# Hybrid decoder step: the last normalization in one pass with early aggregation, its rows stored in 16 pieces of 256 KB by the queues of SyncE and ScalarE in turn

## The reference, cut to what matters

```
def layer_norm(x, g, b):
    xf = x.astype(F32)
    mu = jnp.mean(xf, -1, keepdims=True)
    var = jnp.mean(jnp.square(xf - mu), -1, keepdims=True)
    return ((xf - mu) * lax.rsqrt(var + LN_EPS) * g.astype(F32) + b.astype(F32)).astype(x.dtype)
...
    f, fbuf = conv_ffn(h, ffn_buf, ffn_w_up, ffn_conv_w, ffn_w_down)
    y = layer_norm(DN_ALPHA * h + f, ln2_g, ln2_b)
```

## Time and profile before

| | |
|---|---|
| time, three runs | 2946.45, 2952.71, 2958.77 us; median 2952.71 |
| profiled execution, span | 2947.1 us; the page gives no other time for it |
| TensorE busy in the span | 2788.9 us, 95% |
| VectorE, ScalarE, GpSimd busy | 77%, 47%, 12% |
| the chain that ended last | 49% TensorE, 5% VectorE |

### The profile page before, as it was taken

The page is one execution under the profiler, slowest core; times in us unless marked ns, Lnnn a source line. Parts: engine busy times, 40 slices in busy tenths (PEclk is TensorE's granted clock), DMA queues, the critical chain, the costliest instruction groups (busy, mean ns, idle before and its releaser), DMA issues.

```text
span 2947.1 us, 55566 instructions
## 1 busy us (share of the span) xinstructions
PE 2788.9 (95%) x22685; PEld 2676.0 (91%) x22685; DVE 2278.0 (77%) x3537; ACT 1384.8 (47%) x2371; POOL 359.2 (12%) x332
## 2 busy tenths in 40 slices
PE   8999999999989969999889999999999999999996
PEld 8999999988888658889889999999999999999996
DVE  6656877877657777755688888888888888878898
ACT  4434545545646544522264444444444453434344
POOL 0010000013370315223330000000000000000002
PEclk9999999999989989999999999999999999999998
DMA  7564444448722884563344444444343464434343
GB/s 221 179 206 107 117 119 128 113 150 286 275 82 105 343 247 117 148 175 92 90 157 136 119 126 117 137 115 132 111 141 111 137 194 163 153 112 155 114 124 118
DMA packets 521474, 440.14 MB, mean 149 GB/s; under 512 B 36264, under 2 KB 476767, under 8 KB 515147
## 3 DMA queue, kind: packets, MB, share of 16 engines
q1 hardware_dynamic: 456662, 300.70, 35.6%
...
...
## 4 chain that ended last, share of the span: by engine, by line
PE 49%; DVE 5%; issue 1%; ACT 1%; POOL 1%; DMA 1%; DVEq 0%; ACTq 0%; POOLq 0%
PE i L3363 42%; PE i L140 7%; DVE f_half L3869 1%; DMA x_blocks<-s_blk 1%; POOL x_blocks L3311 1%; DVE x_blocks L3907 1%; DVE h_rows L3902 0%; DVE y_rows L4000 0%; DVE w_ring L3858 0%; DVE x_blocks L3835 0%; PE i L3372 0%; DVE y_rows L3993 0%; DVE f_sum L3862 0%; DVE ln_parts L3913 0%; ACT x_blocks L3657 0%
## 5 line engine op out<-in xcount | busy, mean ns | idle before, releaser
L3363 PE MATMUL i<-x_blocks,f_half 128*128 128x272 f32 x10752 | 1357.0, 288 | 26.0 <-DVE h_rows L3902 10.9
L3363 PEld LDWEIGHTS i<-x_blocks,f_half 128*128 128x128 f32 x10752 | 1347.0, 189 | 31.7 <-DVE x_blocks L3907 14.1
L570 PE MATMUL a<-xb_in,w_half 128*128 128x272 f32 x4200 | 546.9, 291 | 8.9 <-DVE w_half L972 4.6
L570 PEld LDWEIGHTS a<-xb_in,w_half 128*128 128x128 f32 x4200 | 536.0, 190 | 18.2 <-issue 7.2
L3586 ACT CAST f_half<-w_ring 128x1024 fp32r<-128x1024 f32 (+2 forms) x370 | 346.2, 936 | 403.1 <-PE i L3363 339.5
L3869 DVE TENSOR_TENSOR f_half<-w_ring,f_half 128x1024 fp32r<-128x1024 f32 (+2 forms) x362 | 393.4, 1087 | 80.3 <-ACT f_half L3586 77.9
L3869 DVE TENSOR_TENSOR f_half<-f_sum,f_half 128x1024 fp32r<-128x1024 f32 (+2 forms) x148 | 159.5, 1078 | 81.4 <-ACT f_half L3586 81.4
L972 DVE TENSOR_TENSOR w_half<-w_ring,w_half 128x1024 fp32r<-128x1024 f32 x129 | 157.5, 1222 | 82.9 <-ACT w_half L708 82.5
L3586 ACT CAST f_half<-f_sum 128x1024 fp32r<-128x1024 f32 (+2 forms) x148 | 138.8, 938 | 150.1 <-PE i L3363 148.9
L3323 POOL TENSOR_TENSOR f_half<-w_ring,f_half 128x512 fp32r<-128x512 f32 x8 | 12.9, 1611 | 1397.0 <-ACT f_half L3586 1397.0
L708 ACT CAST w_half<-w_ring 128x1024 fp32r<-128x1024 f32 x125 | 131.3, 1050 | 108.9 <-PE a L570 104.8
...
## 6 DMA issues: line engine op xcount, KB each, us to landing
...
```

The costliest lines, as they stand in the source:

```text
L570: last = nc.tensor.matmul(ps[bank][:, 0:HT2], half(q, w)[:, k], XB[v[j]][:, k], start=j in (0, 1, 3) and k == 0 and i == 0, stop=k == HK - ...
L3363: last = nc.tensor.matmul(ps[bank][:, 0:HT2], half(e, j, wl_)[:, s], XB[:, x0 + s, xl_, BLK_OF[j]], start=start and s == 0 and i == 0, sto ...
```

## The change

- Gamma is multiplied into `y_rows` before the statistics are complete, by blocks: GpSimd does it for blocks 0 to 13 (two at a time, 128 x 4 x 256 elements, `times_g` of GpSimd), in pairs 2 to 7 of the last quarter and once after them; VectorE does the last two blocks in the tail. The statistics are taken from the rows before that.
- y = y*gamma*rstd + (beta - mean*rstd*gamma). The bracket is a product of a matrix with six rows: ones, the shift -mean*rstd, and their halves, against beta and gamma and theirs. TensorE makes it, 16 matmuls of 128 x 512 into six PSUM banks, and VectorE needs one pass over the rows (L4066 after). For this the shift is transposed on TensorE (four transposes) and copied by ScalarE, and beta and gamma are loaded as two rows (`BG_RAW`), whose halves GpSimd makes in pair 6 (L3355 and L3357 after, 2 x 2048).
- The first ten blocks' statistics are aggregated during the last pair (`early_moments`), and their result is put back as if it were the statistics of one block (`early_tuples`); the final bn_aggr reads 42 columns and not 96.
- The loads of gamma and beta as broadcast rows go four pairs earlier in SyncE's queue.
- The last transposition writes bank 0 and need not wait for the copy of the one before; the statistics of blocks 12 and 13 are taken earlier in the last pair.
- The 512 prompt rows are stored in 16 pieces of 128 x 512; odd column pieces (`ACT_STORES`) are issued by ScalarE, even ones by SyncE. GpSimd does the sample rows only.

```diff
-            V_GROUPS = [[(t, q) for q in range(4)] for t in range(QT - 1)] + [[(QT - 1, 0), (QT - 1, 1)]]
-            P_UNITS = [(QT, 0), (QT - 1, 1), (QT, 1)]
+            P_XG, E_ROWS = KT - 2, 10
+            ACT_STORES = [(t, q) for t in range(QT) for q in (1, 3)]
+
+            def turn_bank(m):
+                return 6 if m < KT - 1 else 0
...
+                    if g == 3 * HK + 3:
+                        sp.wait_ge(xq, 28)
+                        sp.wait_ge(tout, 32 * (FT // 4))
+                        sp.dma_start(GROW, A["ln2_g"].partition_broadcast(P)[:, 0, :]).then_inc(gr_in, 16)
+                        sp.dma_start(BROW, A["ln2_b"].partition_broadcast(P)[:, 0, :]).then_inc(gr_in, 16)
+                    if g == 3 * HK + 5:
+                        sp.wait_ge(tr, 6)
+                        sp.dma_start(BG_RAW[0:1], A["ln2_b"]).then_inc(bg_in, 16)
+                        sp.dma_start(BG_RAW[1:2], A["ln2_g"]).then_inc(bg_in, 16)
...
+                for t in range(QT):
+                    for q in range(4):
+                        if (t, q) in ACT_STORES:
+                            continue
+                        sp.wait_ge(yr, 4 * t + q + 1)
+                        sp.dma_start(O[0][0, t * P:(t + 1) * P, q * Q4:(q + 1) * Q4], YN[:, t, q * Q4:(q + 1) * Q4]).then_inc(y_out, 16)
...
+                def times_g(m):
+                    cols = slice(m * P, (m + 2) * P)
+                    gp.wait_ge(bst, m + 2)
+                    g = GROW[:, cols].rearrange("p (o n) -> p o n", o=1).broadcast_to((P, QT, 2 * P))
+                    nc.gpsimd.tensor_tensor(YN[:, 0:QT, cols], YN[:, 0:QT, cols], g, ALU.mult).then_inc(xg, 1)
+
                 for e in range(NP):
                     for j in range(7):
                         if on_pool(e, j):
                             gp.wait_ge(hq, 7 * e + j + 1)
                             nc.gpsimd.tensor_tensor(half(e, j, 1), source(e, j), half(e, j, 0).bitcast(F32), ALU.subtract).then_inc(lp, 1)
...
+                    i = e - NU - 3 * HK
+                    if i == 2:
+                        gp.wait_ge(gr_in, 32)
+                    if i >= 2:
+                        times_g(2 * (i - 2))
+                    if i == 6:
+                        gp.wait_ge(bg_in, BI0 + 32)
+                        gp.wait_ge(tr, 10)
+                        nc.gpsimd.tensor_copy(BG[0:2, :], BG_RAW[:, :]).then_inc(bg_hi, 1)
+                        gp.wait_ge(bg_hi, BH0 + 1)
+                        nc.gpsimd.tensor_tensor(BG_LO[:, :], BG_RAW[:, :], BG[0:2, :].bitcast(F32), ALU.subtract).then_inc(bg_lo, 1)
+                times_g(KT - 4)
...
+                pe.wait_ge(cp, KT - 1)
+                pe.wait_ge(sh, SH0 + 1)
+                for t in range(QT):
+                    last = nc.tensor.transpose(ps[6][0:6, t * P:(t + 1) * P], SH_T[:, t, :], ident)
+                last.then_inc(sh_t, 1)
...
+                for u in range(4 * QT):
+                    t, q = u // 4, u % 4
+                    if u >= 6:
+                        pe.wait_ge(yr, u - 5)
+                    nc.tensor.matmul(ps[u % 6][:, :], SH[:, t * P:(t + 1) * P], BG[:, q * Q4:(q + 1) * Q4], start=True, stop=True).then_inc(cs, 1)
...
+                act.wait_ge(sh_t, ST0 + 1)
+                nc.scalar.copy(SH[:, :], ps[6][0:6, :]).then_inc(sh_r, 1)
                 act.wait_ge(nm, NM0 + 1)
...
+                for h in range(2):
+                    y = YN[0:NS, QT, half_cols(h)]
+                    nc.scalar.activation(y, y, ACT.Identity, scale=RD[0:NS, QT:], bias=NMR[0:NS, QT:]).then_inc(nz, 1)
+                for t, q in ACT_STORES:
+                    act.wait_ge(yr, 4 * t + q + 1)
+                    nc.scalar.dma_start(O[0][0, t * P:(t + 1) * P, q * Q4:(q + 1) * Q4], YN[:, t, q * Q4:(q + 1) * Q4]).then_inc(y_out, 16)
...
+                        if not more and n in (2, 3, 4):
+                            early_moments(2 * (n - 2), min(2 * (n - 2) + 2, QT + 1))
+                        if not more and n == 4:
+                            early_tuples()
...
-                        nc.vector.scalar_tensor_tensor(y, y, MV[:, t, 0:1], ps[q][:, :], ALU.subtract, ALU.mult).then_inc(lk1, 1)
...
-                        nc.vector.scalar_tensor_tensor(y, y, RD[:, t:t + 1], ps[4 + q][:, :], ALU.mult, ALU.add).then_inc(yr, 1)
...
+                times_g(P_XG + 1)
+                dve.wait_ge(xg, XG0 + P_XG // 2 + 2)
+                for u in range(4 * QT):
+                    t, q = u // 4, u % 4
+                    y = YN[:, t, q * Q4:(q + 1) * Q4]
+                    dve.wait_ge(cs, CS0 + u + 1)
+                    nc.vector.scalar_tensor_tensor(y, y, RD[:, t:t + 1], ps[u % 6][:, :], ALU.mult, ALU.add).then_inc(yr, 1)
```

More of the change, by code:

```diff
@@ L3914, in parts, with early_moments, early_tuples @@
                     last.then_inc(bst, 1)
+                def early_moments(first, to):
+                    for tt in range(first, to):
+                        r = P if tt < QT else NS
+                        last = nc.vector.bn_aggr(MV[0:r, tt], BS[0:r, tt, 0:E_ROWS])
+                    link.link(last)
+                def early_tuples():
+                    n = float(E_ROWS * P // 2)
+                    for k in (0, 3):
+                        nc.vector.memset(BS[:, :, E_ROWS - 1, k:k + 1], n)
+                        nc.vector.tensor_copy(BS[:, :, E_ROWS - 1, k + 1:k + 2], MV[:, :, 0:1])
+                        nc.vector.tensor_scalar(BS[:, :, E_ROWS - 1, k + 2:k + 3], MV[:, :, 1:2], n, None, ALU.mult)
                 row_sums(0)
@@ L3973, in _ @@
                 add_down(NP - 1, 6)
-                for m in range(KT - 3, KT):
+                for m in range(KT - 2, KT):
                     parts(m)
                 dve.wait_ge(bst, KT)
-                for first, to in ((QT - 1, QT + 1), (0, QT - 1)):
-                    for tt in range(first, to):
-                        r = P if tt < QT else NS
-                        last = nc.vector.bn_aggr(MV[0:r, tt], BS[0:r, tt])
-                    last.then_inc(bst, 1)
-                dve.wait_ge(dev, 2)
@@ L3983, in _ @@
[L3983 to L4000 removed]
+                for tt in range(QT + 1):
+                    r = P if tt < QT else NS
+                    parts_ = BS[0:r, tt].rearrange("p m s -> p (m s)")[:, (E_ROWS - 1) * 6:KT * 6]
+                    last = nc.vector.bn_aggr(MV[0:r, tt], parts_)
@@ new lines, in _, with times_g @@
+                last.then_inc(bst, 1)
+                def times_g(m):
+                    cols = slice(m * P, (m + 1) * P)
+                    g = GROW[:, cols].rearrange("p (o n) -> p o n", o=1).broadcast_to((P, QT, P))
+                    nc.vector.tensor_tensor(YN[:, 0:QT, cols], YN[:, 0:QT, cols], g, ALU.mult).then_inc(xg, 1)
+                dve.wait_ge(gr_in, 32)
+                times_g(P_XG)
+                dve.wait_ge(dev, 2)
+                link.link(nc.vector.reciprocal(RD[:], RD[:]))
```

109 lines of the change are left out of this document (45 added, 64 removed).

## The result

The changed kernel takes 2962.04 us (median of 5 runs, 2956.74 to 2964.74). The kernel before, run beside it, takes 2951.94. The ratio is 1.0031, with a 95% interval of 1.0018 to 1.0044: about 9 us slower, within the 0.5% that the prediction called no change. The forecast was 2961.3.

What follows compares the result with a forecast made beforehand. TensorE was taken to set the pace in the pairs, with VectorE nearly full (1.07 us to spare). Then +13.1 us up to the last bn_stats and -4.5 in the tail gave +8.6 on 2952.7: 2961.3 us, range 2947 to 2970.

Steps and rivals of the forecast that it cites:

- Hold of VectorE's two-input instructions: Pairs 2 to 5: GpSimd's gamma pieces block VectorE instructions with two SBUF inputs; 0.9 us each, +3.6.
- GpSimd gets there first, and holds it: After a pair's bn_stats, GpSimd's gamma piece starts before VectorE's two-input tensor_tensor and delays it: +2.1 us of VectorE time.
- Pair 6 with the clock: Pair 6: gamma piece, copy and subtraction on GpSimd delay product 6, +7.2 us; TensorE's clock drop adds +1.5.
- Pair 7 and the step before the last bn_stats: Pair 7: held instruction and early aggregations, +1.4 us; before the last bn_stats, no wait for ScalarE's copy, -0.6.
- The tail: From the last bn_stats to the span's end: 20.0 us instead of 24.5, -4.5 (bounds -3 and -6).
- They keep up, with nothing to spare: Tail stores: 16 pieces of 256 KB every 0.66 us need 397 GB/s, against the 401 the queues reached.
- about two: End of the tail: microseconds from GpSimd's last store issue, at 17.9, to landing, so the end is near 20.
- rival C: Tail stores don't keep up: 2 KB rows at a tenth less rate, tail 1.5 us longer, 2962.8 us; 8%.
- signs of being wrong: Listed before measuring: those tensor_tensor at 0.67 us throughout, pairs that still take 11.95, or first stores that queue.
- ends last: Tail: GpSimd's sample rows finish near 20 us, after VectorE's side at 18.8, and so set the end.
- Rival A: Pairs: no hold, GpSimd's new pieces cost VectorE nothing; only -0.6 and -4.5 remain, 2947.6 us; 15%.
- rival B: Pairs: slow GpSimd, 1.60 us per 512 columns, gamma pieces 3.2; +16.9 in all, 2969.6 us; 12%.

Runs made afterwards that it cites:

- e1: Changed kernel without GpSimd's seven multiplications by gamma (rows come out without gamma): 2951.8 us, ratio 0.9998.
- e2: Changed kernel with beta's and gamma's halves made on 128 partitions instead of two and brought to their rows through DRAM: 2953.2 us, ratio 0.9999.
- e8: Changed kernel with GpSimd's gamma pieces replaced by memsets into unread rows, three at a time: 2962.1 us, one run.
- e6: Changed kernel with all 16 stores of 256 KB issued by SyncE: 2958.1 us, one run.
- e4: Changed kernel with the 512 rows stored in 8 pieces of 512 KB by SyncE alone: 2959.3 us, ratio 1.0028.
- e10: Changed kernel with 128-partition halves, gamma pieces cut and re-placed, nine SyncE stores, ScalarE scaling half the sample rows before copying the shift: 2947.9 us, ratio 0.9987.
- e11: e10 with the changed kernel's 16 stores of 256 KB by SyncE and ScalarE in turn: 2950.0 us, one run.
- e12: Changed kernel with only ScalarE's order altered: first half of the sample rows scaled before the shift is copied: 2963.2 us, one run.

## Why the prediction was right

The time was 0.7 us off, the sum 0.7, by a mechanism that the runs confirm. Its terms were less exact than their sum, and the pairs' term, 2.4 too high, and the tail's, 1.1 too low, cancelled in part, and 0.5 us ahead of both weren't forecast. A time within 0.7 us is luck besides: the changed kernel's five runs spread over 8 us.

- *Hold of VectorE's two-input instructions:* right in kind (e1, e2, e8). The step "GpSimd gets there first, and holds it" was wrong in place: VectorE's low half got in, and the case that I gave as the alternative, the next one held instead, is what happened. Pairs 2 to 5 cost 2.7, not 3.6: about 0.8 for pair 2's piece (it shows in pair 3's stretch), and about 0.6 for each of the other three.
- *Pair 6 with the clock:* 7.75 instead of 8.7. The cast took 1.89 to 2.35 where I took 3.1. It did hold VectorE, which no row before had shown: 2.19, where the earlier trace rows had it for two-input ones alone. TensorE's wait was 5.87 and the clock's part 1.5 to 1.6, as estimated. That it came out so well is luck in part: after the same wait e6 lost 2.6, more than my bound of 1.9.
- *Pair 7 and the step before the last bn_stats:* +0.30 instead of +0.8; here the 2.4 us piece came ahead of VectorE's low half (2.72), so the hold was real. The early aggregation itself costs nothing, and the earlier statistics win 1.0 rather than 0.6 (e1: 12.73 against 13.73).
- *The tail:* 21.15 instead of 20.0. Up to the first pass 5.4 us instead of 5.85, the 16 passes 10.62 instead of 10.5, GpSimd's last issue at 16.9 instead of 17.9: all near. The mis-sized step is "They keep up, with nothing to spare", and the landing of "about two". The stores move at 356 GB/s on the mean and not at 401, the 4.46 MB take 12.5 us, and the last one lands 4.25 us after its issue. That is rival C's mechanism, near its size (it gave 1.5 more, and the tail is 1.1 longer than forecast); I had it at 8% as an alternative when it came on top of the forecast. Stores that queue were also one of my own signs of being wrong. C's reason, the 2 KB rows, is shown for the best windows only: on the mean, 4 KB rows move faster in e4 (381) and no faster in e10 (340, against e11's 343). That GpSimd's side "ends last" was right by the order of issues and wrong as a cause (e10, e12).
- *In the working itself:* a 0.1 in VectorE's sum has no item behind it, and 6.5+11.3 is 17.8 and not 17.9; neither matters. The cost of a DMA that I took from the Trainium skill ("DMA: Bandwidth & Descriptors", section "Anatomy of one DMA") is given there for DMAs that GpSimd issues, and the store that I set it beside is SyncE's; the sum didn't use it.
- Rival A falls with e1 and e8, rival B with pieces of 2.4 us.

Open: why every kernel that stores from the first pass on ends 15.4 to 16.2 us after it. The mean rate of 340 to 381 GB/s for the 4.46 MB gives 11.7 to 13.1 us of it; what sets the rate, the row length, the sample rows' 32 partitions or something else, wasn't separated. Open too is what makes the clock fall 2.3 us after work stops in one trace and 4.8 in another.
